# Second half of the output weights split inside attention, and the last head pair's query tiles taken from four key tiles down to one

## What is computed

```
h = rms_norm(x, norm1[l]);  proj = h @ w_in[l]
o_a = causal_block_attention(q_a, k_a, v_a)             # group A: latent attention, 4 heads
o_b = sliding_window_attention(q_b, k_b, v_b, sinks)    # group B: window of 128
o_c = dsa_attention(q_c, k_c, v_c, q_idx, k_idx, w_idx) # group C: each query keeps its top 128 keys
o_d = causal_block_attention(q_d, k_d, v_d, log_f_cum)  # group D: forget gates
mixed = concatenate([o_a, o_b, o_c, o_d], axis=-1)      # 512 x 1024
x = x + mixed @ w_out[l]
h2 = rms_norm(x, norm2[l])
x = x + square(relu(h2 @ w_up[l])) @ w_down[l]
```

## Time and profile before

| | us |
|---|---|
| median of three runs | 1926.37 |
| profiled execution, its own time | 1931.15 |
| its span in the profile | 1929.3 |
| PE busy | 1852.3 |
| DVE busy | 912.9 |
| ACT busy | 651.9 |
| POOL busy | 740.5 |

### The profile page before, as it was taken

How to read it: one execution, slowest core, us unless ns; L and a number is a source line. 1 busy time by engine, 2 the same in 40 slices (tenths; PEclk the granted TensorE clock), 3 DMA queues, 4 the chain that set the end, 5 groups by cost and what they waited for, 6 DMA issues and landing times.

```text
span 1929.3 us, 22937 instructions
## 1 busy us (share of the span) xinstructions
PE 1852.3 (96%) x9006; PEld 1476.0 (77%) x9010; DVE 912.9 (47%) x1555; ACT 651.9 (34%) x1172; POOL 740.5 (38%) x326
## 2 busy tenths in 40 slices
PE   7999889999999999998899999999999999999997
PEld 6678557788888886786577888888788888888786
DVE  3667762424141426688624534436521124339374
ACT  4534351322121245343423222212434443443212
POOL 5232243444444443332333544444333233235342
PEclk9999899999999999997999999999999999999999
DMA  7224002232232233120024343343332222322211
GB/s 220 66 66 164 1 1 86 75 103 87 91 105 87 70 94 108 49 83 1 1 66 164 100 157 123 134 154 99 94 127 88 66 66 90 109 66 88 88 66 44
DMA packets 104441, 170.89 MB, mean 89 GB/s; under 512 B 21615, under 2 KB 39431, under 8 KB 103208
## 3 DMA queue, kind: packets, MB, share of 16 engines
q1 hardware_dynamic: 103320, 169.79, 27.0%
q10 hardware_dynamic: 1040, 0.00, 0.0%
HBM read 166.56 MB, written 7.93 MB: 90 GB/s over the span
## 4 chain that ended last, share of the span: by engine, by line
PE 88%; DVE 6%; ACT 2%; issue 2%; POOL 0%; DMA 0%; SPq 0%; DVEq 0%; ACTq 0%
PE G L2010 25%; PE G L2012 25%; PE G L2011 25%; PE S L2272 2%; PE S L1053 1%; DVE neg_max L1882 1%; DVE select L1846 1%; PE G L2308 1%; PE S L2055 1%; ACT prob L1497 1%; PE S L1027 1%; DVE work L1682 1%; PE S L1038 1%; PE G L2289 1%; DVE top L1681 1%
## 5 line engine op out<-in xcount | busy, mean ns | idle before, releaser
L1283 POOL TENSOR_TENSOR w_lo<-raw,w_hi 128x1024 fp32r<-128x1024 f32 x272 | 678.0, 2513 | 1011.2 <-ACT w_hi L1320 688.1
L1320 ACT ACTIVATE w_hi<-raw 128x2048 fp32r<-128x2048 f32 x96 | 183.8, 1915 | 543.7 <-PE G L2012 543.7
L2010 PE MATMUL G<-h_hi,w_hi 128*128 128x512 f32 x896 | 359.9, 402 | 2.1 <-DVE h_lo L810 2.1
L2012 PE MATMUL G<-h_hi,w_lo 128*128 128x512 f32 x896 | 354.8, 396 | 0.0
L2011 PE MATMUL G<-h_lo,w_hi 128*128 128x512 f32 x896 | 354.7, 396 | 0.0
L2010 PE MATMUL G<-w_hi,h_hi 128*128 128x512 f32 (+2 forms) x704 | 281.4, 400 | 6.6 <-issue 4.9
L2012 PE MATMUL G<-w_hi,h_lo 128*128 128x512 f32 (+2 forms) x704 | 272.1, 386 | 0.0
L2011 PE MATMUL G<-w_lo,h_hi 128*128 128x512 f32 (+2 forms) x704 | 271.6, 386 | 0.0
L2012 PE MATMUL G<-w_hi,u_lo 128*128 128x512 f32 x512 | 204.2, 399 | 0.0
L2010 PEld LDWEIGHTS G<-h_hi,w_hi 128*128 128x128 f32 x896 | 168.5, 188 | 45.0 <-DVE h_lo L810 2.9
L2011 PE MATMUL G<-w_lo,u_hi 128*128 128x512 f32 x512 | 201.7, 394 | 0.0
(11 more groups left out here) (314 smaller groups left out, 2247.7 us busy)
## 6 DMA issues: line engine op xcount, KB each, us to landing
raw<-in_w_in_dram SPq DMA_DIRECT2D x40, 1024.0 KB, 5.4
raw<-in_w_up_dram SPq DMA_DIRECT2D x32, 1024.0 KB, 5.3
raw<-in_w_down_dram SPq DMA_DIRECT2D x32, 1024.0 KB, 5.0
raw<-in_w_out_dram SPq DMA_DIRECT2D x12, 1024.0 KB, 5.0
w_ada<-in_w_ada_dram SPq DMA_DIRECT2D x4, 3072.0 KB, 11.9
skew_scratch<-line_scratch SPq DMA_DIRECT2D x1, 4608.0 KB
raw<-in_w_in_dram SPq DMA_DIRECT2D x8, 512.0 KB, 4.5
raw<-in_w_in_dram SPq DMA_DIRECT2D x4, 832.0 KB, 6.7
```

Of the source, the lines that this page charges most:

```text
L1283: ins = pool.tensor_tensor(w_lo[:, c % SPLIT_SLOTS, part], raw[:, c % RAW_SLOTS, part], w_hi[:, c % SPLIT_SLOTS, part].bitcast(F32), ALU.s ...
L1320: act.activation(w_hi[:, c % SPLIT_SLOTS], raw[:, c % RAW_SLOTS], ACT.Copy).then_inc(high_ready, 1)
L2010: pe.matmul(dst, a_hi, b_hi, start=first, stop=False)
L2012: return pe.matmul(dst, a_lo, b_hi, start=False, stop=last)
```

## The change

It has two parts. First, piece 13 is split inside attention: ACT makes its high part in two halves of 1024 columns, in the iterations i = 6 and i = 8, behind `take_probs`; POOL makes its low part in four instructions of 512 columns, behind the scalings of items 9, 10, 11 and 13. The waits for the load and for the freed slot go with it. The old places are gone. Second, `ITEMS` gives the last pair (group C, second pair, items 20 to 23) the tiles 3, 2, 1, 0 instead of 0, 1, 2, 3; TensorE's test for the first item of a pair is by i % TT and no longer by qt.

```diff
 PAIRS = [(g, hp) for g in "DAC" for hp in range(2)]
-ITEMS = [(p, qt) for p in range(len(PAIRS)) for qt in range(TT)]
+
+ITEMS = [(p, TT - 1 - n if p == len(PAIRS) - 1 else n) for p in range(len(PAIRS)) for n in range(TT)]
 NI = len(ITEMS)
...
 MIX_ORDER = (0, 1, 2, 3, 4, 6, 7, 5)
+
+
+MID_HIGH = {6: slice(0, 2), 8: slice(2, 4)}
+MID_LOW = {9: 0, 10: 1, 11: 2, 13: 3}
+MID_PIECE = 2 * (JOB_V + 1) + 1
...
+            def part_low(number, c, k):
+                pool.wait_ge(high_ready, number + 1)
+                ins = pool.tensor_tensor(w_lo[:, c % SPLIT_SLOTS, k], raw[:, c % RAW_SLOTS, k],
+                                         w_hi[:, c % SPLIT_SLOTS, k].bitcast(F32), ALU.subtract)
+                if k == HALF_K - 1:
+                    ins.then_inc(low_ready, 1)
+
...
                 for i in range(NI):
                     scale_probs(i, l * LAYER_SC)
-                for c in range(2 * OUT_JOB + 1, FIRST_GROUP_PIECE):
+                    if i in MID_LOW:
+                        part_low(number + MID_PIECE, MID_PIECE, MID_LOW[i])
+                for c in range(MID_PIECE + 1, FIRST_GROUP_PIECE):
                     split_low(number + c, c)
...
+                def part_high(part):
+                    c = MID_PIECE
+                    act.wait_ge(raw_loaded[c % RAW_SLOTS], l * LAYER_LOADS[c % RAW_SLOTS] + loads_upto(c))
+                    act.wait_ge(bank_filled, (jobs + PROJ_JOBS) * TT)
+                    ins = act.activation(w_hi[:, c % SPLIT_SLOTS, part], raw[:, c % RAW_SLOTS, part], ACT.Copy)
+                    if part.stop == HALF_K:
+                        ins.then_inc(high_ready, 1)
+
...
                     if i:
                         take_probs(i - 1)
-                    if i == NI - 1:
-                        ahead(JOB_V, 1)
+                    if i in MID_HIGH:
+                        part_high(MID_HIGH[i])
...
-                    if qt == 0:
+                    if i % TT == 0:
                         turns_taken(QK_NO[p, qk_units(p) - 1])
```

## The result

The changed kernel takes 1913.83 us (median of four runs, 1912.45 to 1915.56), the kernel before 1926.43 (four runs, 1924.74 to 1927.21): ratio 0.9933, 95% interval 0.9921 to 0.9945, or 12.6 us. Forecast were 1916.6, and 1911.5 to 1922.0 as the range. A second measurement beside other kernels gave 1915.57 and 0.9928 (0.9911 to 0.9944).

What follows compares the result with a forecast made beforehand. TensorE bounds the kernel, with a 2.44 us hole before each layer's output product. Both parts together save 4.9 us a layer, 9.8 in two, taking the median from 1926.37 to 1916.6 us; range 1911.5 to 1922.0.

Steps and rivals of the forecast that it cites:

- The collision: Before the output product, DVE's fourth split of the mixed output runs beside POOL's piece 13 split: about 2.15 us a layer.
- The walk of the last pair: Step-by-step timing of items 20 to 23, widest first, from 269.04: product starts at 286.15 instead of 291.08, 4.9 us a layer.
- the front: Start of the last pair, wide item 20 behind wide item 19: item 23's scores at 278.8 instead of 277.62, costing 1.2 us.
- The parts in attention cost nothing: ACT's half-parts in items 6 and 8 and POOL's after items 9, 10, 11, 13 fit idle time: cost nothing.
- the slower rival: Parts in items 6 to 13 lie on attention's chain, adding up to 7.3 us a layer: 1931.2 us; chance 0.05.
- That doubt: In mid attention, one top-k mark (L1686) per layer could meet a POOL part, at up to 1.3 us a layer.
- The clock rival: TensorE keeps 2.4 GHz through the output product's start, saving 3.2 us more: 1913.4 us; chance 0.20.
- The weak rival: At items 19 and 20 the front costs 4 us, leaving only the collision's 2.2 us a layer: 1922.0 us; chance 0.13.
- alone it is worth 2.2 us: Moving piece 13's split from attention's end, without the new order, since TensorE's own value products end nearly as late.
- everything behind: All work after the output product's start is TensorE's, so its length was taken to stay unchanged.

Runs made afterwards that it cites:

- the bunched one: Changed kernel with ACT's high part as one instruction in item 8 and POOL's four low parts in one row behind item 11: 1916.69 us, ratio 0.9944.

## Why the prediction was right, and where it was not

**The collision** was read rightly: POOL's split stood on DVE's fourth split. With POOL waiting and all else in place the start comes 2.57 and 2.14 us sooner; I had 2.15.

**The walk of the last pair** held in nearly each step. Rows of the changed kernel, TensorE's timeline for the earlier trace rows and ACT's exponentials of item 20:

```profile
277.21 0.49 PE L2295 MATMUL S<-qkT 64*128 64x128 f32 x4
```

```profile
271.08 0.69 ACT L1512 ACTIVATE prob<-S,neg_max 128x512 f32<-128x512 f32 x1 [1.08 <-DVE neg_max L1905]
```

Item 20's exponentials come 2.80 us behind item 19's, forecast 2.8. Item 22's scores start 6.14 us behind them, forecast 6.2. Item 23's scores come 8.93 us behind item 19's exponentials, and 8.02 before: the front costs 0.91 us, where I had 1.2. From there to the product it is 7.19 us, where I had 7.3. Together 5.36 us a layer instead of 4.9, 10.7 instead of 9.8. The step that was a little off is one burst of TensorE, from item 22's scores (274.42) to item 23's (277.21): 2.79 us, where the walk has 3.0. The walk lets its four operations follow each other in full; in the trace each begins some 0.07 us before the one ahead is over, as the row of 1.09 us stands in the chain for 1.02. Four times that would be the 0.25 us; this is an estimate from these rows.

**The parts in attention cost nothing**, as forecast. ACT's and POOL's timelines in the changed kernel:

```profile
226.65 1.06 ACT L1535 ACTIVATE w_hi<-raw 128x1024 fp32r<-128x1024 f32 x1
227.59 0.37 ACT L1512 ACTIVATE prob<-S,neg_max 128x128 f32<-128x128 f32 x1
...
231.89 1.06 ACT L1535 ACTIVATE w_hi<-raw 128x1024 fp32r<-128x1024 f32 x1
```

```profile
244.38 1.27 POOL L1295 TENSOR_TENSOR w_lo<-raw,w_hi 128x512 fp32r<-128x512 f32 x1
245.61 0.61 POOL L1305 TENSOR_TENSOR prob<-prob,inv_sum 128x256 f32<-128x256 f32 x1
...
249.38 1.27 POOL L1295 TENSOR_TENSOR w_lo<-raw,w_hi 128x512 fp32r<-128x512 f32 x1
```

The parts take 1.06 and 1.27 us (forecast 1.05 and 1.3). The followers start at once behind them, 0.1 us later for item 8's exponentials (forecast 0.3) and 0.3 us later for item 12's scaling (forecast 0.4), counted from the items before. Items 7 to 11 take 15.32 to 15.34 us and items 11 to 15 take 13.87 to 13.89 in every profile but the bunched one's, with spread parts as without any. Bunched, they cost 0.75 us: so the slower rival was a real mechanism, and the spread over four items is what kept it away. The Trainium skill (SBUF — State Buffer, Who interferes with whom) says that copies and tensor_scalar in a two-port mode can take the pair that GpSimd needs. That doubt was not put to the test for the marks of the top-k: the one near the parts starts at 252.46, 1.8 us behind the end of the last. MAX8 and MATCH_REPLACE8 beside the parts keep their 0.68 us. The load of piece 17 goes out at 250.93 instead of behind 290.43, and no wait in the profile comes of it.

**The clock rival** came in half. I gave the full effect (both layers' first halves at 2.4 GHz) a chance of 0.20, as a case apart, and left it out of the sum. In both profiles of the changed kernel one layer of two keeps the clock. Filling the holes of before shows that the effect is there and is worth 1.54 us a layer, so in the sum it belonged as a term: the hole costs its length and, some of the time, a slower start of what follows. The walk leaves 2.45 us from the end of item 22's products (283.7) to the product (286.15), and the text says 1.1 us without work; the trace has 0.84 and 1.01, with item 23's 0.44 us of value products between. In the profiles the chain gives 10.7 us and the clock about 1.6, near the 12.6 measured; how often the other executions kept the clock is not known. The forecast of 9.8 us was thus low by 0.9 in the walk and by a term that was priced, but left out of the sum.

**The weak rival was mis-priced.** I took removal of the collision alone for 4.4 us in all. The two kernels that do only that have ratios of 0.9944 and 0.9946, 10.8 and 10.4 us, at least 6.6 by the intervals; their chain accounts for 4.2 and 4.7, their first halves for 2.5 and 3.1. For the product's start "alone it is worth 2.2 us" was about right (1.7 to 2.6); the step that failed is that it stood for the whole, since "everything behind" did not stay: the first halves sped up by 1.0 to 1.6 us each. What is left, 4.1 and 2.6 us by the ratios and nothing at the low end of the intervals, was not found in one place: the other stretches differ in steps of about 1.5 us between profiles of one kernel, and whether a shorter hole shifts these in a lasting way stays open.

## What to carry to other kernels

Ask of an "issue" hole on the bound engine what each other engine is doing, and of a strangely long DVE instruction with two SBUF inputs what POOL runs beside it; then a wait on POOL can be worth as much as moving its work. Where a pipeline ends in a product that depends on its last item, try the narrowest item last: here that was worth 2.8 to 3.2 us a layer once the collision was gone. A hole ahead of dense matmuls costs its own length, and here up to 1.5 us of slower clock behind it; count both.

## What the runs showed of the hardware that I had not expected

- Identity transposes in TensorE's holes kept the granted clock at 2.4 GHz: 2.93 busy us of 4 instead of 1.75 in the like stretch, then 1.00 granted instead of 0.60 from 284 to 288, and the product's first half in 11.53 us instead of 13.07, with the kernel 2.7 to 8.7 us faster for more work.
- DVE's two splits and POOL's two subtractions take 5.29 and 5.10 us side by side, against 1.28 and 4.72 apart. DVE takes four times as long, POOL 8% longer; the lengths fit taking turns, an instruction each.
- The same stretch of the same kernel takes one of two values some 1.5 us apart (changed kernel, items 15 to 19: 12.5 or 14.0 us, at a mean granted clock of 1.00 or 0.88), so two single profiles can differ by 6 us more than the medians do.
